# Gate and up projections of four fp32 FFNs as seven quarter products instead of eight, on one Trainium2 core

## What is computed

```python
for layer in range(2):
    g = norm_gains[layer]
    h = h + 0.5 * swiglu(rmsnorm(h, g[0]), w_gate[layer, 0], w_up[layer, 0], w_down[layer, 0])
    u = rmsnorm(h, g[1])
    h = h + (even_mixer(u, ...) if layer % 2 == 0 else odd_mixer(u, ...))
    h = h + 0.5 * swiglu(rmsnorm(h, g[2]), w_gate[layer, 1], w_up[layer, 1], w_down[layer, 1])
return rmsnorm(h, final_norm)[:, 16:]

def swiglu(h, w_gate, w_up, w_down):          # 1024 -> 2816 -> 1024
    return (silu(h @ w_gate) * (h @ w_up)) @ w_down
```

## Time and profile before

| | us |
|---|---|
| median of 3 runs | 1982.86 (1982.52 to 1983.92) |
| the profiled execution | 1984.11 |
| its span, first to last instruction | 1982.3 |
| TensorE busy | 1946.1 |
| VectorE busy | 900.7 |
| ScalarE busy | 599.7 |
| GpSimd busy | 58.4 |

### The profile page before, as it was taken

One profiled execution on the slowest core, in us unless ns is written; L12 is line 12 of the kernel. 1 busy time (PEld: TensorE's weight loads), 2 busy tenths in 40 slices (PEclk: granted clock), 3 DMA queues, 4 the chain that ended last, 5 costly groups with the idle time before them and its releaser, 6 DMA issues.

```text
span 1982.3 us, 33974 instructions
## 1 busy us (share of the span) xinstructions
PE 1946.1 (98%) x14030; PEld 1842.2 (93%) x14030; DVE 900.7 (45%) x1141; ACT 599.7 (30%) x810; POOL 58.4 (3%) x64
## 2 busy tenths in 40 slices
PE   6999999999999999999999999999999999999997
PEld 6999999999899999999999999999998888888885
DVE  5444443346655444443344444333556654444333
ACT  5222222224324222222232222222423332222221
POOL 0000000000000000000000000000034000000001
PEclk8999999999999999999999999999999999999998
DMA  4323223332122322323332222233322233233331
GB/s 166 110 85 93 87 81 95 90 124 65 43 71 82 96 92 87 93 78 97 91 93 88 86 94 84 87 88 97 98 65 65 81 93 95 92 95 91 94 91 42
DMA packets 53122, 175.72 MB, mean 89 GB/s; under 512 B 6524, under 2 KB 8860, under 8 KB 52928
## 3 DMA queue, kind: packets, MB, share of 16 engines
q1 hardware_dynamic: 52816, 174.71, 28.9%
q10 hardware_dynamic: 240, 0.07, 0.0%
HBM read 171.35 MB, written 3.41 MB: 88 GB/s over the span
## 4 chain that ended last, share of the span: by engine, by line
PE 96%; DVE 2%; ACT 1%; DMA 0%; issue 0%; SPq 0%; DVEq 0%; ACTq 0%
PE psum L1070 92%; DVE wl L699 1%; DMA raw<-in_w_gate_up 0%; PE psum L1185 0%; ACT wh L384 0%; PE psum L1230 0%; PE psum L1092 0%; PE psum L1318 0%; PE psum L1206 0%; DVE ss L709 0%; PE psum L1231 0%; DVE x L1059 0%; ACT sq L399 0%; PE psum L1184 0%; PE psum L1207 0%
## 5 line engine op out<-in xcount | busy, mean ns | idle before, releaser
L1070 PE MATMUL psum<-xh,wh 128*128 128x264 f32 (+1 forms) x3024 | 701.7, 302 | 7.8 <-DVE xl L716 7.8
L1070 PE MATMUL psum<-xl,wh 128*128 128x264 f32 (+1 forms) x3024 | 699.4, 301 | 0.0
L1070 PE MATMUL psum<-xh,wl 128*128 128x264 f32 (+1 forms) x3024 | 697.4, 301 | 0.0
L384 ACT ACTIVATE wh<-raw 128x1024 fp32r<-128x1024 f32 x255 | 270.1, 1060 | 880.7 <-PE psum L1070 878.2
L699 DVE TENSOR_TENSOR wl<-raw,wh 128x1024 fp32r<-128x1024 f32 x327 | 404.9, 1238 | 258.4 <-ACT wh L444 155.6
L1070 PEld LDWEIGHTS psum<-xh,wh 128*128 128x128 f32 x3024 | 487.1, 189 | 28.3 <-DVE wl L699 7.8
L1070 PEld LDWEIGHTS psum<-xl,wh 128*128 128x128 f32 x3024 | 485.7, 189 | 18.4 <-issue 0.5
L1070 PEld LDWEIGHTS psum<-xh,wl 128*128 128x128 f32 x3024 | 485.0, 189 | 17.7
L1070 PE MATMUL psum<-hh,wh 128*128 128x264 f32 (+1 forms) x1424 | 335.2, 303 | 1.5 <-DVE hl L885 1.5
L1070 PE MATMUL psum<-hh,wl 128*128 128x264 f32 (+1 forms) x1424 | 334.8, 303 | 0.0
L1070 PE MATMUL psum<-hl,wh 128*128 128x264 f32 (+1 forms) x1424 | 334.7, 303 | 0.0
(11 more groups left out here) (207 smaller groups left out, 691.9 us busy)
## 6 DMA issues: line engine op xcount, KB each, us to landing
raw<-in_w_gate_up SPq DMA_DIRECT2D x176, 512.0 KB, 3.6
raw<-in_w_down SPq DMA_DIRECT2D x64, 448.0 KB, 3.3
raw<-in_w_down SPq DMA_DIRECT2D x32, 512.0 KB, 3.5
raw<-in_od_in SPq DMA_DIRECT2D x21, 512.0 KB, 3.6
raw<-in_ev_in SPq DMA_DIRECT2D x18, 512.0 KB, 3.7
raw<-in_ev_out SPq DMA_DIRECT2D x8, 512.0 KB, 3.6
raw<-in_od_out SPq DMA_DIRECT2D x8, 512.0 KB, 3.6
x<-in_x_t SPq DMA_DIRECT2D x8, 264.0 KB, 5.9
```

The lines of the kernel that those rows point to most:

```text
L384: act.activation(wh[:, slot, :], raw[:, slot, :], ACT.Copy).then_inc(wh_ready, 1)
L1070: last = pe.matmul(dst, weights[:, slot, w], moving[:, k, tok], start=start and p == 0, stop=stop and p == 2)
```

## The change

**Seven products.** The pair's weights (K halves by gate/up) and the input (K halves by token halves) are split into quarters; Winograd's form of Strassen's method gives the four output quarters with 7 products for 8. Each product is 4 channel tiles x 3 passes = 12 matmuls of 264 (or 256) columns into one bank. The weight quarters a, b (gate), c, d (up) enter as a, b, d and four sums e, f, g, h, which VectorE makes (`sum_ef`, `sum_g`, `sum_h`); high parts by ScalarE (`high_ab`, `high_sum`, `high_d`), low parts by VectorE (`low_ab`, `low_gh`, `low_ef`, `low_d`). The 7 input operands (bh, bl) are made tile by tile, with the gain in them, by `operands` on both engines in place of xh and xl; the mixers' in-projections keep xh and xl. Output sums are formed in PSUM: ScalarE copies ("seeds") one bank into the next, and later products accumulate on it.

```diff
-def from_x(n, tile, ...):   # 48 matmuls per tile, two tiles per pair
+def next_pair(q, s, p, i=0):            # TensorE, one window per pair
+    wait g1_ready (p >= 2), low_ready (w + 1)
+    product(BANK_X[p % 2], OP_P1, high a, low a, True)         # chunk_done d + 1
+    finish_pair(name, p - 1, i)         # S4 -> Z (waits low_d, seed_z), d + 2; Q2 -> W (waits seed_w), d + 3
+    wait low_ready (w + 2), seed_y
+    product(BANK_Y[p % 2], OP_S2, g, False)                    # d + 4
+    wait low_ready (w + 3), v_kept
+    product(BANK_V, OP_V1, e, True)                            # d + 5
+    product(BANK_X[p % 2], OP_Q1, b, False)                    # d + 6
+    wait seed_z
+    product(BANK_Y[p % 2], OP_S3, f, False)                    # d + 7
+def product(bank, op, w_high, w_low, real, start, ready=None):
+    for k in range(4):
+        for p, (weights, moving) in enumerate(((w_high, bh), (w_high, bl), (w_low, bh))):
+            last = pe.matmul(psum[:, bank, 0:width(real)], weights[:, w], moving[:, op, k, 0:width(real)], ...)
```

```diff
-    if n >= RING:
-        sp.wait_ge(wl_ready, lap * RING + n - RING + 1)
-    sp.dma_start(raw[:, slot, 0:cols], src)
+    slot_free(n)      # chunk: chunk_done of n - 4; gate: Q1 of pair p - 2; up: low_d of pair p - 2
+    sp.dma_start(raw32[:, n % RING, 0:cols], src)
...
-    dve.tensor_tensor(wl[:, slot, :], raw[:, slot, :], f32(wh[:, slot, :]), ALU.subtract)
+    dve.tensor_tensor(raw[:, n % RING, 0:w], raw32[:, n % RING, 0:w], f32(high_of(n % RING)[:, 0:w]), ALU.subtract)
```

More of the change, by code:

```diff
@@ L350, in _ @@
             for s in range(8, EV_TILES):
-                load(CHUNK["ev_in"] + s, ev_in[s])
-            for s in range(KT):
-                load(CHUNK["ev_out"] + s, ev_out[s])
+                load(LOAD["ev_in"] + s, ev_in[s])
+            for s, m in enumerate(MORDER):
+                load(LOAD["ev_out"] + s, ev_out[m])
             ffn_loads(1)
@@ L362, in _ @@
             for s in range(8, OD_TILES):
-                load(CHUNK["od_in"] + s, od_in[s])
-            for s in range(KT):
-                load(CHUNK["od_out"] + s, od_out[s])
+                load(LOAD["od_in"] + s, od_in[s])
+            for s, m in enumerate(MORDER):
+                load(LOAD["od_out"] + s, od_out[m])
             ffn_loads(3)
@@ new lines, in window @@
+            def window(q, s, p, i=0, last=False):
+                name = f"up{q}{s}"
+                if not (p == 0 and q == 0 and s == "a"):
+                    low_gh(name, p, i)
+                if p:
+                    up_second(name, p - 1, i)
+                if not (p == 0 and q == 0 and s == "a"):
+                    low_ef(name, p, i)
+                if not last:
+                    sum_ef(name, p + 1, i)
+                    sum_g(name, p + 1, i)
+                if p:
+                    up_first(name, p - 1, i)
+                if not last:
+                    sum_h(name, p + 1, i)
+                if p:
+                    gate_second(name, p - 1, i)
+                low_d(name, p, i)
+                if p:
+                    product(name, p - 1, i)
+                if not last:
+                    low_ab(name, p + 1, i)
+                else:
+                    low(LOAD[f"down{q}{s}"])
+                if p:
+                    hidden_low(name, p - 1, i)
+                if last:
+                    low(LOAD[f"down{q}{s}"] + 1)
+                if p == 0 and s == "a":
+                    v = {0: 0, 1: 2, 2: 3, 3: 5}[q]
+                    mean(v, 2, real_from(name))
+                    inverse_root(v, real_from(name))
+                gate_first(name, p, i)
@@ L811, in _ @@
+            sum_ef("up0a", 0)
+            sum_g("up0a", 0)
+            sum_h("up0a", 0)
+            low_ab("up0a", 0)
+            for m in range(4, KT):
+                dve.wait_ge(x_in[m], 16)
+                gained(gate, 0, 0, m - 4)
+                sum_q(0, 0, m - 4)
+                low_q(0, 0, m - 4)
+                if m == 5:
+                    low_gh("up0a", 0)
+                if m == 6:
+                    low_ef("up0a", 0)
             for m in range(KT):
                 add_square(0, m)
-            dve.wait_ge(table_ready, 2)
@@ L1369, in odd_ready @@
                     pe.wait_ge(yd_l, k - 3)
[L1370 to L1372 removed]
+            for o in range(KT):
+                mixed("od_out", o, odd_ready, real=True)
+            ffn(3)
             pe.wait_ge(acc_free, TILES)
```

1092 lines of the change are left out of this document (741 added, 351 removed).

## The result

The changed kernel takes **1999.4 us** (median; 1997.7 to 2003.0) against 1983.4 in the same comparison, a ratio of 1.0085 with a 95% interval of 1.0071 to 1.0099: slower by 0.85%. The forecast was 1.5% slower (2013 us, range 1979 to 2055).

A forecast was written before the change was run, and what follows sets the result against it. The prediction took TensorE, busy for 98% of the span, to bound the kernel. Its terms summed as 1982.3 - 122.6 + 86 + 30 + 12 + 25 = 2012.7, so about 2013 us, range 1979 to 2055.

The forecast's parts named there:

- The matmuls that go: In the FFNs' gate and up pairs, fewer matmuls remove 96.7 us in the first three and 25.9 in the last: 122.6.
- Rival B: In the pair loops, writing a single bank in a row costs 6.6 ns a matmul, giving 2050 us; chance 7%.
- The pair loop: VectorE's and ScalarE's circle of waits, 9.87 us, fits TensorE's 10.26 us window: price zero, upper bound 58 us.
- Rival A: VectorE or its circle with ScalarE bounds the pair loop, giving 2035 to 2070 us; chance 22%.
- Pass starts: At the eight FFN pass starts TensorE waits for VectorE's and ScalarE's lists: 86 us, bounds 43 and 105.
- the clock: Lower granted clock after new gaps: 14 us in ev_in and 11 at four pass starts, +25 us, bounds 0 and 40.
- V1's wait: At a first pass's start, TensorE idles before product V1 for VectorE's operands and low parts: 8.9 us from ffn1 to ffn2.
- seed_z: In a first pass's first window, this ScalarE seed stands behind the root and a table load: TensorE idles 4.3 us.
- the late silu of the second window: In a first pass, the second window loses another 1.5 us to ScalarE's late silu.
- The start of the program: Before ffn0's first full window, VectorE's list and eight square sums delay TensorE: 24 us of the pass starts' cost.
- Rival C: Pass starts cost half, 86 becoming 43, and 11 us of clock go, giving 1959 us; chance 12%.
- The mixers: Raw slots free later, so steps wait for loads: 30 us in ev_in with ev_out, 12 in od_in; bounds 20 and 60.

The follow-up runs named there:

- experiment 4: Changed kernel with one unused VectorE multiplication added per pair-loop window: 2018.8 us with 528 elements, 2052.2 us with 1024.
- Experiments 1 and 2: Changed kernel with rounding and low part of the chunk four ahead moved to the step's end: in ev_in 1960.7 us, in od_in as well 1945.6 us.
- experiment 3: Changed kernel with 32 matmuls that nobody reads added ahead of the transposes of eight ev_in steps, step order unchanged: 1991.5 us.

## Why the prediction was right, and where it wasn't

**The matmuls that go.** 122.6 us were expected, from 0.1221 us for 264 columns and an estimated 0.1186 for 256. Both numbers stand in the chain after, so this term is met. Rival B, a price for writing one bank in a row, is out: 960 matmuls in 117.22 us are no slower than the 3168 alternating ones of the earlier trace rows. The formula for the gap in the Trainium skill (TensorE: Matmul & The Clock Gate, Back-to-back issue gap) gives 112.5 ns for 264 columns, an estimate; no loop of any run here shows it, and the row decided rightly.

**The pair loop.** Price zero, with 9.87 us against 10.26, was right; the circle measured 9.80. Rival A, at 22%, is out by the loops without a break and by experiment 4. What carried this step was reading the distance between starts instead of the recorded durations: without it the circle came to 11.06 us, and the forecast to 2070. Experiment 4 shows the distance in a loop that VectorE's circle bounds: over the 9.81 us of the changed kernel's own catching-up windows, 528 elements cost 0.61 us and 1024 cost 1.13, the distances of the earlier trace rows (0.62, 1.14) and not the durations (0.71, 1.22). The bound of rival A was priced too high at its lower end: halfway to no overlap the circle would be 10.47 us, 0.2 above 10.26, which over 72 windows is 15 us and not 29. And the 5.3 us that VectorE had per pair before are in recorded durations; by distances, as the 9.0 of now are counted, they were 4.8. By the rule that the next instruction starts when the pipe is empty, quoted in the prediction from the Trainium skill (VectorE: DVE Perf Modes, The DRAIN you can't avoid), the loop would have been VectorE's. The same section adds that an instruction that isn't held starts earlier; this the prediction left out, and by it page and trace agree.

**Pass starts.** This term was too large. 86 us and 11 of clock were charged to the starts; the FFNs lost 122.6 us of matmuls, of which 40.0 arrived, so the starts cost 82.6 with the clock in it. The three items of a first pass, by the trace of the third FFN's: V1's wait, 8.9 expected, 7.0 measured; seed_z, 4.3 expected, 2.3 measured; the late silu of the second window, 1.5 expected, and nothing of it is to be seen. That is 5.4 us; taken for each of three passes it is 16 us and covers the 14.4 that the term was too large. It is read from one pass: seed_z is 2.2 to 2.3 in all of them, but V1 waits for 8.0 us at the second FFN, and at the fourth for 2.5 behind the 4.1 us wait ahead of its first matmul. For seed_z the working itself was wrong, and the trace of the changed kernel shows how (ScalarE's timeline):

```profile
1042.69 1.28 ACT L556 ACT_TABLE_LOAD   x1
1044.59 0.64 ACT L556 ACTIVATE rms<-rms 128x528 f32<-128x528 f32 x1 [0.61 <-DVE rms L1052]
1045.14 0.37 ACT L589 ACTIVATE psum<-psum 128x264 f32<-128x264 f32 x1
```

The table load stands ahead of the root's wait, not behind it: ScalarE loads the table while it waits for VectorE's mean, so its 1.28 us are hidden. The prediction had put them into the chain. The start of the program, 24 expected, is the one that was met: ffn0 lost 32.2 - 2.8 = 29.4 us, against 27.5 and its part of the clock. Rival C, half of the 97 us, did not come; 83 is well above its 55.

**The mixers.** 30 and 12 us, and 14 for the clock, 56 in all; measured 52.9. The mechanism is the one described: slot freed by the last matmul, load, high, low, attention. Experiments 1 and 2 take it away, and all but about 1 of the 53 us with it. Split by mixer it was 44 against 37.7 and 12 against 15.2. Of the 44 the clock had 14, and experiment 3 gives 13.6: this term was met, and the waiting was the one too large. A step of ev_in took 15.2 us where 13 were named: that number started from the 9.8 us of one fast step, not from the mean of 11.05, and left the clock out. The difference to before is 4.1 us a step, of which 1.9 are the clock's and 2.2 waiting, where up to 2.3 and 3.0 were expected; and the wait came in seven steps, not eight.

**The sum.** The span was put 16.8 us too high: 14.4 in the FFNs (25.6 less expected, 40.0 measured), 3.1 in the mixers, and 0.7 the other way at the end. So most of the miss is in the pass starts, by the reading above in their three items.

**What the prediction didn't ask.** It took the order of the mixers' steps as given and priced it. The same argument, a list whose head waits for a load that is needed four steps later, says that the head belongs at the end, and this was worth 54 us, more than the change itself brings in the FFNs.

## What to carry to other kernels

When a change makes a buffer live longer (here low weights that overwrite the raw ones), look at every list that has the refill at its head: move it behind what the same step still owes to others, and the later load need not cost anything (here about 1 us of 53 was left). An engine's room in a loop can be measured by adding one instruction of known length to its list: if the time between windows becomes constant, what is left of it after subtracting the added piece is the length of the circle. The matmuls that went were worth 122.6 us here, and the serial work of the other engines at eight starts took 83 of them; count the starts before the loops. A filler for a wait belongs only where the trace shows the wait: in the one place without one it cost 4.7 us.

## What the runs showed of the hardware that I had not expected

- Matmuls that do nothing but fill a wait made the kernel faster, twice: 32 in each of seven waits of 3.9 to 5.3 us, and in one place without a wait, gave 7.9 us, and 234 at four starts 6.5 us, as the granted clock behind them rose from 0.50 to 1.00.
- In the loops that VectorE's circle bounds, the windows repeat to within 0.02 us (10.42, 10.94).
- The load of a 512 KB chunk landed in 3.4 to 3.5 us (medians) in the mixers and in 3.5 in the FFNs' loops.
- ScalarE loaded its table (1.28 us) ahead of a wait that lasted 0.61 us beyond it, so that the load cost nothing there.
